# Latent tokens gather U and V of a pick as one row of 8 KB; dots, GELU, weights and V sums follow two rows at a time

## The chip, the cores and the metric

One core of a Trainium2 chip. The metric is the device time of one execution in microseconds, the median of the runs.

## What is computed

One inference step of a hybrid backbone with two layers, on 128 context tokens and 256 latent tokens of width 1024, all in float32. Each layer has token mixers (pooling, a two-way state scan, differential attention) and then PEER expert retrieval: every token picks 128 experts (8 heads of 16) of 16384 by product keys, reads for each pick a row of U and a row of V of 4 KB each, and adds a gated sum to its state.

```
act = jnp.einsum("td,thkd->thk", xb, u_tab[ib])
return jnp.einsum("thk,thkd->td", jax.nn.gelu(act) * gb, v_tab[ib])
```

The rows read for this are 3 tiles of 128 tokens x 128 picks x 2 layers x 8 KB, 805 MB in all; the weights, keys and inputs are 163 MB more.

## The kernel before

The program runs four steps k = 0 to 3: context of layer 0, latents of layer 0 (two tiles of 128 tokens), context of layer 1, latents of layer 1. Each step has a dense part (projections, mixers, attention, output projection, query projection `wq`), then the choosing of the picks (`choose` on DVE: MAX8, FIND_INDEX8, MATCH_REPLACE8, lines 1460 to 1566), which ends in the index tables `idx` and `vidx`. The gathers of a step run beside the dense part and the choosing of the next step, those of the last step alone at the end.

A **U gather** (line 695, GpSimd, called POOL here) takes column r of `idx`: 128 rows of 4 KB, partition p getting the row for pick r of token p. DVE then multiplies it with `h_kept` (the 128 hidden states of the tile, copied to PSUM at line 1866) and sums along the row (line 1871), which gives one column of `dots`. After 64 columns ACT applies GELU (line 1367) and DVE multiplies with the gates into `wv`, regrouped in 16 pieces (line 1882).

A **V gather** uses `vidx`, in which the index table is regrouped (line 1571, 16 copies of 32x32) so that the four quarters of the partitions hold four picks of the same 32 tokens. For 16 such gathers DVE spreads the weights over a 128x512 tile `vw` (line 1852); PE then multiplies each gathered tile, in two halves of 512 columns, with a 128x32 slice of `vw` (line 1077). Four gathers of a unit belong to four groups of 32 tokens, so that their outputs lie in the four lanes of 32 partitions of `acc[0]` and `acc[1]`. After all 128 picks DVE adds `acc` to x (lines 1895 to 1900), which lets the next layer begin.

A matmul in float32 appears as two MATMUL records; a 128x512 one of line 1077 as two records of 128*32, 128x512.

The order of all this is written out: a plan (`gather_plans`) gives each pause of the dense part a list of events. For the latents `events_two` interleaves "u" (4 U gathers), "v" (4 V gathers, 19 units behind) and "g", "w", "s", "x" for the GELU, the weights, the `vw` tile and the end. Every engine walks the same list between its dense pieces, and POOL issues the gathers in that order. Each gather goes to a slot of 4 KB per partition: 10 in `ring`, and others where other buffers are free, so that beside the context step of layer 1 there are 17, and at the end 34 and more. A slot is given again only after its last user: a U slot after its dot (`u_used`), a V slot after its two matmuls (`v_used`).

```
if held_before[n] is not None:
    before = stream[held_before[n]]
    pool.wait_ge(u_used if before[0] == "u" else v_used, used_after[before])
table, at = (io["peer_u"], idx) if kind == "u" else (io["peer_v"], vidx)
```

SyncE (SP) loads the weight chunks of 2 MB, 16 KB per partition, on its own queue.

## Time and profile before

| | us |
|---|---|
| median of 3 runs | 2434.72 |
| lowest and highest | 2434.61, 2435.57 |
| span of the profiled execution | 2689.8 |
| PE, DVE, POOL, ACT busy in the profile | 1510.1, 1524.4, 1466.1, 281.3 |

The profile gives the span from the first to the last instruction and no time of its own for what lies around it. The profiled execution is 255 us longer than the median. The page slices its span in 40 parts with the busy share of the engines and of the 16 DMA engines; a share of DMA somewhat above 1.00 can stand in a short window, since packets are counted with their overlap.

### The profile page before, as it was taken

The numbers are of one execution on the slowest core, as the hardware profiler recorded it, in microseconds if no ns is written. First come the engines' busy times: TensorE is split into PE (matmuls) and PEld (weight loads), VectorE is DVE, ScalarE is ACT, GpSimd is POOL, SyncE is SP. The second block draws the span as 40 slices with busy tenths as digits, with TensorE's granted clock in tenths as the row PEclk, the third lists the DMA queues.
The fourth block names the chain that finished last, engine by engine and source line by source line (L and its number), as shares of the span: only waits on it lengthen the run. The fifth ranks groups of instructions, "written<-read, shape, count | busy, mean of one in ns | idle before, by whom it ended". The sixth has DMA issues, their size and how long they took to land.

```text
span 2689.8 us, 20637 instructions
## 1 busy us (share of the span) xinstructions
PE 1510.1 (56%) x6676; PEld 682.0 (25%) x6676; DVE 1524.4 (57%) x4059; ACT 281.3 (10%) x715; POOL 1466.1 (55%) x1540
## 2 busy tenths in 40 slices
PE   6898668694244554554556866868400444442466
PEld 2464433371012110122312442354100100110012
DVE  0349974756886555455360965575776844446401
ACT  1321133010000110100000032211000000000000
POOL 0005445536665666666556635545676666667664
PEclk8889888896666665676768787878755655565568
DMA  9979998988999999999979988888899999999997
GB/s 360 411 320 379 395 388 324 365 306 318 357 397 411 412 388 379 371 410 411 389 286 374 364 341 314 324 313 296 318 399 373 343 383 375 358 374 383 378 357 271
DMA packets 238044, 969.43 MB, mean 360 GB/s; under 512 B 26314, under 2 KB 28746, under 8 KB 227954
## 3 DMA queue, kind: packets, MB, share of 16 engines
q0 software_dynamic: 221184, 805.40, 78.0%
q1 hardware_dynamic: 16754, 162.71, 14.9%
q8 instruction: 54, 0.88, 0.1%
q14 instruction: 52, 0.43, 0.0%
HBM read 964.87 MB, written 3.15 MB: 360 GB/s over the span
## 4 chain that ended last, share of the span: by engine, by line
DVE 27%; PE 24%; issue 15%; POOL 13%; another core or an unknown queue 11%; DMA 7%; ACT 2%; SPq 0%; DVEq 0%; ACTq 0%; POOLq 0%
PE acc L1077 8%; PE psum L1031 6%; DVE ring L1871 6%; POOL work L695 6%; POOL ring L695 5%; DVE work L1871 3%; PE psum L786 3%; DVE work L1463 2%; POOL wring L695 2%; DMA ring<-peer_v_in,vidx 2%; PE psum L796 2%; DVE work L1460 2%; DMA ring<-peer_u_in,idx 1%; DVE wring L1871 1%
## 5 line engine op out<-in xcount | busy, mean ns | idle before, releaser
L695 POOL DMA_INDIRECT ring<-peer_u_in,idx x415 | 396.5, 955 | 460.6 <-DVE idx L1566 208.0
L1871 DVE CUSTOM_DVE_ANT_0 ring<-ring,h_kept 128x1024 f32<-128x1024 f32 x415 | 488.9, 1218 | 126.3 <-DMA ring<-peer_u_in,idx 93.5
L695 POOL DMA_INDIRECT ring<-peer_v_in,vidx x392 | 378.5, 966 | 325.8 <-PE acc L1077 116.9
L1077 PE MATMUL acc<-ring,vw 128*32 128x512 f32 x1412 | 299.2, 778 | 276.6 <-DVE vw L1852 107.6
L1077 PE MATMUL acc<-work,vw 128*32 128x512 f32 x852 | 218.4, 794 | 325.5 <-DVE vw L1852 155.0
L1871 DVE CUSTOM_DVE_ANT_0 work<-work,h_kept 128x1024 f32<-128x1024 f32 x220 | 262.0, 1219 | 159.3 <-DMA work<-peer_u_in,idx 124.2
L695 POOL DMA_INDIRECT work<-peer_v_in,vidx x267 | 252.0, 944 | 144.8 <-issue 74.0
L695 POOL DMA_INDIRECT work<-peer_u_in,idx x220 | 207.1, 941 | 116.7 <-issue 58.9
L1031 PE MATMUL psum<-work,wring 128*128 128x256 f32 (+1 forms) x896 | 187.1, 369 | 49.5 <-issue 46.6
L786 PE MATMUL psum<-wring,work 128*128 128x512 f32 (+1 forms) x432 | 180.4, 575 | 32.4 <-issue 22.8
L1031 PEld LDWEIGHTS psum<-work,wring 128*128 128x128 f32 x896 | 160.3, 216 | 81.5 <-issue 62.0
L1077 PEld LDWEIGHTS acc<-ring,vw 128*32 128x32 f32 x1412 | 59.9, 127 | 461.5 <-issue 366.6
L1077 PEld LDWEIGHTS acc<-work,vw 128*32 128x32 f32 x852 | 45.6, 130 | 474.1 <-issue 426.1
L1119 ACT ACTIVATE work<-psum 128x512 f32<-128x512 f32 (+3 forms) x224 | 92.8, 428 | 684.3 <-remote 320.8
L786 PEld LDWEIGHTS psum<-wring,work 128*128 128x128 f32 x432 | 83.9, 211 | 130.2 <-issue 118.5
L1871 DVE CUSTOM_DVE_ANT_0 wring<-wring,h_kept 128x1024 f32<-128x1024 f32 x68 | 81.4, 1220 | 54.8 <-DMA wring<-peer_u_in,idx 25.1
L1460 DVE MAX8 work<-work 128x8 f32<-128x128 f32 (+1 forms) x288 | 52.5, 253 | 103.5 <-ACT work L1119 93.0
L1007 PE MATMUL psum<-wring,work 128*128 128x512 f32 x192 | 88.5, 622 | 3.2 <-ACT work L1294 3.2
L774 PE MATMUL psum<-const,hn 128*128 128x128 f32 x96 | 18.4, 357 | 116.8 <-DVE hn L1448 75.4
L1077 PE MATMUL acc<-ring,work 128*32 128x512 f32 x156 | 55.0, 794 | 49.0 <-issue 32.3
L695 POOL DMA_INDIRECT wring<-peer_u_in,idx x68 | 66.9, 983 | 25.7 <-issue 20.1
L796 PE MATMUL psum<-work,wring 128*128 128x256 f32 (+1 forms) x288 | 61.1, 369 | 31.5 <-issue 17.0
(244 smaller groups left out, 2028.4 us busy)
## 6 DMA issues: line engine op xcount, KB each, us to landing
wring<-w_in_in SPq DMA_DIRECT2D x17, 2048.0 KB
wring<-peer_wq_in SPq DMA_DIRECT2D x14, 2048.0 KB
wring<-mod_w_in SPq DMA_DIRECT2D x10, 2048.0 KB
ring<-mod_w_in SPq DMA_DIRECT2D x9, 2048.0 KB, 12.2
wring<-w_out_in SPq DMA_DIRECT2D x8, 2048.0 KB
work<-mod_w_in SPq DMA_DIRECT2D x5, 2048.0 KB, 14.4
ring<-peer_u_in,idx POOLq DMA_INDIRECT x415
ring<-peer_v_in,vidx POOLq DMA_INDIRECT x392
```

Source lines behind the costliest of these rows:

```text
L695: nc.gpsimd.indirect_dma_start(slots[slot_of[n]], None, table, bass.IndirectOffsetOnAxis(ap=at[:, col + r:col + r + 1], axis=0))\
L774: ins = tr(p[:, i * P:(i + 1) * P], hn[st.X + t][:, b * P:(b + 1) * P], ident)
L786: ins = mm(p[:, 0:n], st.L.hT[0][:, b, t * P:(t + 1) * P], w[:, b, slot:slot + n], start=(b == 0), stop=(b == DB - 1))
L796: ins = mm(p[:, 0:st.N], w[:, b, i * P:(i + 1) * P], st.L.hT[0][:, b, 0:st.N], start=(b == 0), stop=(b == DB - 1))
L1007: ins = mm(p[:, :], st.L.catT[:, b, t * P:(t + 1) * P], chunk("wo", k, cc)[:, b, :], start=(b == 0), stop=(b == DB - 1))
L1031: ins = mm(p[:, 0:N], chunk("wq", k, b // 4)[:, kb, (b % 4) * P:(b % 4 + 1) * P], st.L.hT[1][:, kb, 0:N], start=(kb == 0), stop=(kb == DB ...
L1077: ins = mm(acc[half][lane:lane + QUAD, :], w[:, at:at + QUAD], two[j - pair][0][:, half * CHUNK:(half + 1) * CHUNK], start=(r == 0), stop= ...
L1119: A(dst, src, ACT.Copy, scale=scale).then_inc(*take(*key))
L1460: d(V.max(top[:, b * TOPK + 8 * r:b * TOPK + 8 * r + 8], values[:, b * width:(b + 1) * width]))
L1463: d(V.max_index(index[:, b * TOPK + 8 * r:b * TOPK + 8 * r + 8], top[:, b * TOPK + 8 * r:b * TOPK + 8 * r + 8], values[:, b * width:(b + 1 ...
L1871: V.tensor_tensor_reduce(held, held, h_kept[:, :], 1.0, 0.0, ALU.mult, ALU.add, dots[:, dots_at(k, t) + r:dots_at(k, t) + r + 1]).then_inc ...
```

## The change

The tables U and V lie interleaved in HBM as `peer_uv`, and are seen as rows of 4 KB (`peer_one`) or as rows of 8 KB that hold U and V of one expert (`peer_both`). Context tokens go on as before with rows of 4 KB, with doubled indices. Latent tokens use a new kind of gather, "f": 128 rows of 8 KB, in a wide slot of two neighbouring old slots, indexed by `vidx`, in which now 32 columns in turn belong to one group of 32 tokens (`by_group`). A gather so holds four picks of each of the 32 tokens of a group. For the dots the hidden states of the group have to lie in all four quarters: PE spreads them by a matmul with a repeated unit matrix (`spread_h`, event "h", once in 32 gathers). Two gathers (DUO) are handled together: two dots, a GELU on 128x2 (event "e"), the weights and a `vw` piece of 128x64 (event "m", `weigh`), and four matmuls (event "p"), which take the two halves of each row to two lanes of `acc`. The event order for a tile is now f(2i), m(i-1), p(i-1), f(2i+1), e(i). A wide slot is given again after its matmuls.

Core of the diff (what is left out are the changes of names, of constants' layout and of the wide-slot bookkeeping):

```diff
+DUO = 2
+DUOS = PICKS // DUO
+VW_DUOS = SHARE // DUO
+BESIDE_CHOOSING, BEHIND_CONTEXT = 13, 10
...
+        wide = {n: ring[:, n * D:(n + 2) * D] for n in range(0, RING, 2)}
...
+        spare_line(region(10288, 3 * D), 3, after_step[STEPS - 3], after_step[STEPS - 2])
+        spare_line(region(10288 + 3 * D, 4 * D), 4, after_step[STEPS - 3], row_no["u", STEPS - 2, 0, 0])
+        spare_line(region(2 * D, 8 * D), 8, after_step[STEPS - 2], row_no["u", STEPS - 2, 0, 0])
+        for held in wring:
+            spare_line(held, DB * CHUNK // D, row_no["f", STEPS - 1, 0, 0], len(stream))
+        spare_line(region(0, 16 * D), 16, after_step[STEPS - 1], len(stream))
...
+                if kind == "f" and r == 0:
+                    pool.wait_ge(*after("both_indexed", k, t))
...
+                for before in (stream[m] for m in held_before[n]):
                     pool.wait_ge(u_used if before[0] == "u" else v_used, used_after[before])
-                table, at = (io["peer_u"], idx) if kind == "u" else (io["peer_v"], vidx)
+                at = idx if kind == "u" else vidx
                 nc.gpsimd.indirect_dma_start(
-                    slots[slot_of[n]], None, table,
+                    row(kind, k, t, r)[0], None, io["peer_both" if kind == "f" else "peer_one"],
...
+            def spread_h(k, t, g):
+
+                pe.wait_ge(u_used, dotted_before["f", k, t, g * QUAD])
+                if g == 0:
+                    pe.wait_ge(*after("h2", k, t))
+                group = slice(g * QUAD, (g + 1) * QUAD)
+                for half in range(2):
+                    o = slice(half * CHUNK, (half + 1) * CHUNK)
+                    ins = mm(h_kept[:, o], c("quads")[group, :],
+                             hn[steps[k].X + t][group, o], start=True, stop=True)
+                ins.then_inc(*mark("h_spread", k, t, g))
...
+                if kind == "p":
+                    if i == 0:
+
+                        pe.wait_ge(*after("acc_free", *previous_tile(steps, k, t)))
+                    pe.wait_ge(*after("vw", k, t, i))
+                    for j in range(DUO):
+                        r = i * DUO + j
+                        g, held = r // QUAD, row("f", k, t, r)[0]
+                        for half in range(2):
+                            lane = QUAD * ((g + 2 * half) % 4)
+                            ins = mm(acc[half][lane:lane + QUAD, :], vw_duo(i)[:, j * QUAD:(j + 1) * QUAD],
+                                     held[:, D + half * CHUNK:D + (half + 1) * CHUNK],
+                                     start=(r % QUAD == 0), stop=(r % QUAD == QUAD - 1))
+                        ins.then_inc(v_used, 1)
...
+                if kind == "e":
+                    at = dots_at(k, t) + i * DUO
+                    act.wait_ge(u_used, dotted_before["f", k, t, (i + 1) * DUO - 1] + 1)
+                    A(dots[:, at:at + DUO], dots[:, at:at + DUO], ACT.Gelu_apprx_tanh).then_inc(*mark("gelu", k, t, i))
...
+            def weigh(k, t, i):
+
+                at, place = dots_at(k, t) + i * DUO, slice(i * DUO, (i + 1) * DUO)
+                dve.wait_ge(*after("gelu", k, t, i))
+                d(V.tensor_tensor(wv[:, place], dots[:, at:at + DUO], gates_of(k, t)[:, place], ALU.mult))
+                settle()
+                if i >= VW_DUOS:
+                    dve.wait_ge(v_used, used_after["f", k, t, (i - VW_DUOS + 1) * DUO - 1])
+                else:
+                    dve.wait_ge(v_used, sums_of(*previous_tile(steps, k, t)) if t == 0 else
+                                used_after["f", k, t - 1, PICKS - (VW_DUOS - 1 - i) * DUO - 1])
+                spread_out = [P, DUO, QUAD]
+                V.tensor_tensor(vw_duo(i).rearrange("p (g t) -> p g t", t=QUAD), quad.unsqueeze(1).broadcast_to(spread_out),
+                                wv[:, place].unsqueeze(2).broadcast_to(spread_out), ALU.mult).then_inc(*mark("vw", k, t, i))
...
+                elif kind == "f":
+                    held, landed, count = row("f", k, t, i)
+                    dve.wait_ge(landed, count)
+                    at = dots_at(k, t) + i
+                    V.tensor_tensor_reduce(held[:, 0:D], held[:, 0:D], h_kept[:, :], 1.0, 0.0, ALU.mult, ALU.add,
+                                           dots[:, at:at + 1]).then_inc(u_used, 1)
+                elif kind == "m":
+                    weigh(k, t, i)
...
+    events = []
+    for n in range(st.T * DUOS + 1):
+        t, i = divmod(n, DUOS)
+        before = (st.k, *divmod(n - 1, DUOS))
+        if t < st.T:
+            if i * DUO % QUAD == 0:
+                events.append(("h", st.k, t, i * DUO // QUAD))
+            events.append(("f", st.k, t, i * DUO))
+        if n:
+            events += [("m", *before), ("p", *before)]
+        if n and n % DUOS == 0:
+            events.append(("x", st.k, t - 1, 0))
+        if t < st.T:
+            events += [("f", st.k, t, i * DUO + 1), ("e", st.k, t, i)]
+    return events
+
+
+EARLY = 30
...
-            dots = max(n for n, event in enumerate(left) if event[0] == "u") + 1
-            most = dots + int((len(left) - dots) * ROOM)
+            ends = [n + 1 for n, event in enumerate(left) if event[0] == "p"]
+            dots, most = ends[-1 - BESIDE_CHOOSING - BEHIND_CONTEXT], ends[-1 - BEHIND_CONTEXT]
```

### Where instructions move

POOL, gathers of the latents of layer 0 beside the dense part of the next context step. Before (`ring` and `work` are the slots):

```order
L695 DMA work<-peer_u_in,idx 128x1024 [waits u_used] x3
L695 DMA work<-peer_v_in,vidx 128x1024 [waits u_used]
L695 DMA work<-peer_v_in,vidx 128x1024 [waits v_used] x3
L695 DMA ring<-peer_u_in,idx 128x1024 [waits v_used]
L695 DMA ring<-peer_u_in,idx 128x1024 [waits u_used] x3
L695 DMA ring<-peer_v_in,vidx 128x1024 [waits u_used]
L695 DMA ring<-peer_v_in,vidx 128x1024 [waits v_used] x3
```

and now:

```order
L734 DMA ring<-peer_uv_in,vidx 128x2048 [waits v_used,both_indexed]
L734 DMA ring<-peer_uv_in,vidx 128x2048 [waits v_used] x4
L734 DMA work<-peer_uv_in,vidx 128x2048 [waits v_used] x3
L734 DMA ring<-peer_uv_in,vidx 128x2048 [waits v_used] x5
L734 DMA work<-peer_uv_in,vidx 128x2048 [waits v_used] x3
```

Rows of 128x1024 in 17 slots have become rows of 128x2048 in eight wide ones (five in `ring`, three in `work`), and each waits for `v_used`, so for matmuls, where every second run of four waited for `u_used` alone.

DVE, choosing in the context step of layer 1 (lines 1460 to 1502 before, 1531 to 1579 now, are the choosing itself). Before:

```order
L1882 TENSOR_TENSOR wv<-dots,gates 32x16 [waits v_step,gelu]
L1882 TENSOR_TENSOR wv<-dots,gates 32x16 x15
L1852 TENSOR_TENSOR vw1<-const,wv 128x512 [waits v_used,v_step]
L1460 MAX work<-work 128x8 x16
L1463 MAX_INDEX work<-work 128x8 [waits v_step]
L1463 MAX_INDEX work<-work 128x8 x15
L1495 TENSOR_TENSOR work<-work,const 128x256 [waits v_step]
L1502 TENSOR_TENSOR work<-work 128x8x16
```

and now, the same stretch:

```order
L1531 MAX work<-work 128x8 x16
L1534 MAX_INDEX work<-work 128x8 [waits v_step]
L1534 MAX_INDEX work<-work 128x8 x15
L1940 TENSOR_TENSOR wv<-dots,idx 128x2 [waits gelu,v_step]
L1948 TENSOR_TENSOR vw0<-const,wv 128x64 [waits v_used,v_step]
L1968 ISA ring,dots<-ring,h_kept 128x1024 [waits row_landed8]
L1968 ISA dots 128x1
L1968 ISA ring,dots<-ring,h_kept 128x1024 [waits row_landed0]
L1968 ISA dots 128x1
L1940 TENSOR_TENSOR wv<-dots,idx 128x2 [waits gelu]
L1948 TENSOR_TENSOR vw0<-const,wv 128x64 [waits v_used,v_step]
...
L1572 TENSOR_TENSOR work<-work,const 128x256
L1579 TENSOR_TENSOR work<-work 128x8x16
```

The choosing had only the weights of V units between its pieces; now it has dots (line 1968), weights (1940) and `vw` pieces (1948) of 13 duos.

PE, in the dense part of the same step, V sums between two projections. Before:

```order
L1077 MATMUL acc0<-work,vw0 32x512 [waits row_landed14,row_landed13]
L1077 MATMUL acc0<-work,vw0 32x512
L1077 MATMUL acc1<-work,vw0 32x512 x2
L1077 MATMUL acc0<-work,vw0 32x512 [waits row_landed16,row_landed15]
```

and now:

```order
L1122 MATMUL acc0<-work,vw0 32x512 [waits vw]
L1122 MATMUL acc1<-work,vw0 32x512
L1122 MATMUL acc0<-work,vw0 32x512
L1122 MATMUL acc1<-work,vw0 32x512
L1122 MATMUL acc0<-ring,vw0 32x512 [waits vw]
L1122 MATMUL acc1<-ring,vw0 32x512
L1122 MATMUL acc0<-ring,vw0 32x512
L1122 MATMUL acc1<-ring,vw0 32x512
```

A unit of four gathers was eight matmuls that filled four lanes in turn; a duo is four matmuls that alternate between two lanes, and it waits for `vw` each time instead of for the landing of rows.

## Rows read from the trace of the kernel before

**Rows 1.** The page's parts 1 to 3, whole span.
```profile
span 2689.8 us, 20637 instructions
...
PE 1510.1 (56%) x6676; PEld 682.0 (25%) x6676; DVE 1524.4 (57%) x4059; ACT 281.3 (10%) x715; POOL 1466.1 (55%) x1540
...
DMA  9979998988999999999979988888899999999997
...
q0 software_dynamic: 221184, 805.40, 78.0%
q1 hardware_dynamic: 16754, 162.71, 14.9%
```

**Rows 2.** Windows: stretch, its length, busy us per engine, clock, DMA share, GB/s.
```profile
core 0: us, PE busy (x) PEld busy (x) DVE busy (x) ACT busy (x) POOL busy (x), PEclk, DMA share, GB/s
70.00:100.00 30.00, 25.99 (x173) 14.14 (x171) 10.55 (x49) 12.86 (x27) 0.00 (x0) 0.94 1.01 430
690.00:1300.00 610.00, 289.61 (x1243) 119.72 (x1242) 371.53 (x743) 49.40 (x128) 391.40 (x413) 0.64 1.00 393
1334.00:1400.00 66.00, 30.17 (x182) 7.71 (x176) 51.49 (x264) 2.76 (x5) 34.34 (x35) 0.72 0.83 310
1400.00:1456.00 56.00, 43.41 (x152) 15.18 (x150) 3.36 (x11) 4.10 (x10) 37.99 (x41) 0.86 0.95 359
1480.00:1940.00 460.00, 326.14 (x1414) 180.40 (x1418) 309.41 (x950) 80.70 (x205) 231.36 (x241) 0.80 0.85 323
1985.00:2015.00 30.00, 0.00 (x0) 0.00 (x0) 18.21 (x30) 0.00 (x0) 22.69 (x25) 0.50 1.03 409
1940.00:2690.00 750.00, 284.65 (x1056) 65.42 (x1048) 371.68 (x691) 3.70 (x8) 487.37 (x513) 0.60 0.94 363
```

**Rows 3.** DMA view, 70 to 100 us: loads of 16 KB rows by SP.
```profile
DMA packets 883, 12.89 MB, mean 430 GB/s; under 512 B 96, under 2 KB 96, under 8 KB 96
```

**Rows 4.** DMA view, 1985 to 2015 us: gathers alone.
```profile
DMA packets 3372, 12.28 MB, mean 409 GB/s; under 512 B 376, under 2 KB 376, under 8 KB 3371
```

**Rows 5.** Timeline of POOL, 2232 to 2243 us: start, duration.
```profile
2234.67 0.94 POOL L695 DMA_INDIRECT work<-peer_v_in,vidx  x1 [0.30 <-issue]
2241.14 0.94 POOL L695 DMA_INDIRECT work<-peer_v_in,vidx  x1 [5.54 <-issue]
```

**Rows 6.** Waits, 2000 to 2690 us: total, times, longest.
```profile
POOL work L695 <- remote: 47.4, 17, 6.1
```

**Rows 7.** DVE groups in the choosing, 1334 to 1400 us: busy, mean ns.
```profile
L1571 DVE COPY vidx<-idx 32x32 uint32<-32x32 uint32 x16 | 3.0, 188 | 0.5
L1882 DVE TENSOR_TENSOR wv<-dots,gates 32x16 f32<-32x16 f32 x16 | 2.9, 180 | 0.6
L1852 DVE TENSOR_TENSOR vw<-const,wv 128x512 f32<-128x512 f32 x3 | 2.1, 692 | 0.1
```

**Rows 8.** Timeline of DVE: dots that follow one another.
```profile
2225.88 1.22 DVE L1871 CUSTOM_DVE_ANT_0 work<-work,h_kept 128x1024 f32<-128x1024 f32 x1
...
2227.16 1.22 DVE L1871 CUSTOM_DVE_ANT_0 wring<-wring,h_kept 128x1024 f32<-128x1024 f32 x1
```

**Rows 9.** DVE groups, whole span, nearest to a 128x64 product.
```profile
L1502 DVE TENSOR_TENSOR work<-work 128x64 f32<-128x64 f32 (+6 forms) x35 | 5.7, 228 | 0.0
```

**Rows 10.** Gathers issued from 1334 to 1456 us.
```profile
L695 POOL DMA_INDIRECT work<-peer_v_in,vidx x38: 935/941/1293, 1334.1 to 1444.9; - x38
L695 POOL DMA_INDIRECT ring<-peer_v_in,vidx x36: 937/941/2171, 1342.9 to 1454.5; - x36
```

**Rows 11.** V sums on PE, 854 to 860 us: ns min/median/max.
```profile
L1077 PE MATMUL acc<-ring,vw x20: 592/592/1062, 854.4 to 858.4; 128*32 128x512 f32 x20
```

**Rows 12.** Timeline of PE: two projections of the context step.
```profile
757.37 15.67 PE L786 MATMUL psum<-wring,work 128*128 128x512 f32 x32 [2.20 <-issue]
```

**Rows 13.** ACT: the GELU and its table loads, whole span.
```profile
L1367 ACT ACT_TABLE_LOAD x8 | 10.3, 1283 | 0.1
...
L1367 ACT ACTIVATE dots<-dots 128x64 f32<-128x64 f32 x12 | 3.1, 257 | 588.5 <-issue 445.2 <-DVEq L1876 143.3
```

More of the change, by code:

```diff
@@ L348, in dots_at, with vw_duo, gates_of @@
             return (sum(st.T for st in steps[:k]) + t) % 2 * PICKS
-        vw_places = [held[:, :] for held in vw] + [region(16384 + i * CHUNK, CHUNK) for i in range(2)]
         def vw_of(k, t, q):
-            return vw_places[q % (4 if k == STEPS - 1 else 2)]
+            return vw[q % 2]
+        def vw_duo(i):
+            at = i % VW_DUOS * DUO * QUAD
+            return vw[0][:, at:at + DUO * QUAD]
+        def gates_of(k, t):
+            at = (steps[k].X + t) * PICKS
+            return idx[:, at:at + PICKS].bitcast(F32)
         def job(pe, *key):
@@ L1354, in gather @@
             def gather(kind, k, t, i):
[L1355 removed]
+                if t == 0 and (kind, i) in (("v", (PICKS - SHARE) // UNIT), ("p", (PICKS - SHARE) // DUO)):
                     if k:
@@ L1861, in gather @@
                 col = n * PICKS
-                if kind == "u":
+                if kind == "h":
+                    if i == 0:
+                        dve.wait_ge(*after("picked", k, t))
+                        settle()
+                        by_group(lambda out, j, m: d(V.tensor_copy(out, gates[QUAD * j:QUAD * (j + 1), col + m:col + PICKS:4])),
+                                 gates_of(k, t), 0)
+                        settle()
+                    dve.wait_ge(*after("h_spread", k, t, i))
+                elif kind == "f":
[6 more added lines that the diff above has]
+                    weigh(k, t, i)
+                elif kind == "u":
                     if i == 0:
```

140 lines of the change are left out of this document (68 added, 72 removed).

## The prediction

> **What bounds the kernel now.** I read the page first: the DMA engines are at 9 tenths in nearly all 40 slices, PE, DVE and POOL at 55 to 57%, ACT at 10%, and of 969 MB the gathers (queue q0) are 805 [rows 1]. So bytes over the DMA rate is the first thing to price. The windows then say where that holds [rows 2]. Beside the dense part of the layer 1 context step (690 to 1300 us) DMA is at 1.00 and moves 393 GB/s: bound by DMA. While that step chooses its picks (1334 to 1400) it is at 0.83, and after it at 0.95. From 1480 to 1940, the dense part of the last step, it is at 0.85 with PE at 326 of 460 us: bound by the dense chain, which starts when the latents of layer 0 are summed. From 1940 on (the latents of layer 1, nothing beside them) it is at 0.94 with 363 GB/s. So time taken out of the layer 0 latents brings the last step forward, and time taken out of the last gathers brings the end forward; both are on the path.
>
> The profiled execution is 2689.8 us, the median 2434.72. At the mean rate of the runs (969 MB in 2435 us, 398 GB/s) DMA has few idle stretches left, fewer than the profile shows. I work out the change from the profile's durations and set it against both.
>
> **Packets.** SP's loads run at 430 GB/s: 883 packets, 787 of them of 8 KB or more, 12.89 MB, so 16 KB each [rows 3]. Gathers of 4 KB rows alone run at 409 GB/s [rows 4]. The ratio is 1.051. I read it as a fixed part per packet: a 16 KB packet carries a quarter of that part per byte, so three quarters of it are 5.1% and all of it is 6.8% of the time of 4 KB; 8 KB takes away half, 3.4%. The latents' rows are 4 tiles x 128 gathers x 128 rows x 8 KB = 537 MB, 1313 us at 409 GB/s. **-45 us**, between 0 (if a row goes as two packets) and -64 (if 8 KB moves like 16 KB). A wide gather then takes 1.049 MB / 423 GB/s = 2.48 us, two old ones 2.56.
>
> What the page on DMA of the Trainium skill (DMA: Bandwidth & Descriptors, SWDGE vs HWDGE vs iDMA) says speaks against this term: a packet is preferably at most 4096 B. By that rule the term would be 0. The 16 KB packets [rows 3] don't keep to it on SP's queue; for POOL's queue no row shows it, and I keep it as a rival.
>
> **POOL.** It issues a gather every 1.24 us (0.94 and 0.30 between) and DMA moves 4 KB rows in 1.28, so it never gets far ahead, and after a pause such as the one of 5.54 us [rows 5] nothing is queued. Pauses of this kind fall on 17 waits, 47.4 us, in the last 690 us [rows 6]. Half as many issues let POOL run ahead to the limit of the slots. The median has no room for many such pauses, so I credit **0** here, with -40 as the far end.
>
> **Choosing in the layer 1 context step.** The order puts 13 duos of dots and weights between its pieces on DVE; before it had 16 weight products and 3 `vw` tiles, 2.9 + 2.1 = 5.0 us [rows 7]. A duo is two dots at 1.28 (2225.88 to 2227.16) [rows 8], a weight product of 0.18 as in [rows 7], a 128x64 `vw` piece of 0.23 by the nearest form [rows 9], and some 0.3 for the two waits between them: 3.3 us. So the 66 us become 66 + 43 - 5 = 104, in which only 26 wide gathers, 64 us, come free. Behind it stand 20 more, 8 of them prefetched; 12 x 2.48 = 30 us. 134 us from the start of the choosing to the first gather of the next step. Before, 38 + 36 gathers were issued from 1334.1 to 1454.5, and the next step's first at 1456: 122 us [rows 10]. **+12 us**, between 0 (if the 14 us in which DVE was idle there [rows 2] take up the dots) and +38 (all that DVE gains in work).
>
> **Slots.** Beside the dense part there were 17 slots, a turn of 17 x 1.28 = 21.8 us. A unit of four V gathers holds its first slot for 3 x 1.28 us and a PE unit (16 records of 592 ns in four lanes, 2.4 us [rows 11]): some 6 us. A U slot is held for one dot. Now 8 wide slots give a turn of 19.8 us, and the first gather of a duo waits for its partner (2.5), for the first gather of the next duo (2.5), a dot (1.3), GELU and weights (1.0) and PE: eight records of 592 ns in two lanes are 2.4 us, at the lower clock (records of 1062 ns, [rows 11]) 4.2. That is 10 to 11 us. What DVE or PE may be away without a gap in DMA falls from some 14 to some 8 us (a POOL issue taken off both). A projection is 7.8 us (two in 15.67, [rows 12]), just inside; at the lower clock, or with a wait for ACT before it, it is not. I take one gap of 1 us at some 10 of the 20 pauses: **+10 us**; the ends are 0 and 20 x 2.3 = +45.
>
> **Small terms.** The first gather of a latent tile now waits for `vidx`, 3.0 us of copies [rows 7]; twice, and at the 0.85 of the last step's windows about half of it shows: +3 (0 to +6). At the end the last gather is followed by dot, GELU, weights and a PE duo (1.3 + 0.4 + 0.7 + 2.4) where one PE unit of 2.4 stood: +3. The 16 spreads of h are four records of some 0.6 us each on PE; DVE waits for them about 3 us once in 32 gathers, while it works 3.3 us of each 4.96: 0. GELU goes from 12 calls of 64 columns to 256 of 2 and 4 of 64, at 0.26 us or less, and the order has ten more table loads of 1.28 us [rows 13]: 13 us on an engine that is 10% busy, 0, at most +5. PE needs 2.4 to 4.2 us for a duo of 4.96, so it hides; without any sharing of lanes at the lower clock a duo would be 8 x 1.06 = 8.5 us, but where PE was busy 26 of 30 us the granted clock was 0.94, and 0.50 where it did nothing (70 and 1985 us in [rows 2]); at the upper one that duo is 4.7.
>
> **Sum:** -45 + 0 + 12 + 10 + 3 + 3 = -17 us. On the median 2435 - 17 = **2418 us**; the profiled span would be near 2673.
>
> **The rivals.**
> *A, the forecast*, 2400 to 2429 us: 0.42.
> *B, the gain is larger*: POOL's headroom brings back idle DMA time beside the packet gain. For it: 6% of 750 us are idle in the last stretch [rows 2], 45 us, with 34 slots to run ahead in. Against it: the runs are 255 us shorter than the profile, so most of that idle belongs to the profiled execution. With 35 us of it: 2383 us. 0.17.
> *C, slower, slots turn too slowly*: place, the dense part of the layer 1 context step and its choosing. Each of some 20 pauses of PE or DVE costs 2.3 us (+45 in place of +10), and the dots in the choosing cost 25 in place of 12: -45 + 45 + 25 + 6 = +31, 2466 us. It decides from the point where a wide slot is held for more than about 12 us and DMA falls below 0.93 in that stretch. For it: every wide slot waits for PE, where half the old ones waited for a dot. Against it: DMA at 1.00 there with PE at 290 and DVE at 372 of 610 us. 0.23.
> *D, it does not do what it says*: POOL cuts the 8 KB rows in packets of 4 KB. The waits stay and the packet gain is gone: +28, 2463 us. For it only the page's rule above. 0.05.
> *E, gain and waits cancel* within 5 us: 2435 us. 0.13.
>
> A measurement of this kernel can tell about 0.2%, 5 us, from no change. Faster by more: A and B, **0.59**; within it: E, **0.13**; slower: C and D, **0.28**. The likeliest is A, so **2418 us**. Its own range is 2400 to 2429; for 8 in 10 the range goes down to B's value and up to most of C's, 2380 to 2460.
>
> **What would show it.** In the profile after: POOL near 1024 indirect DMAs, 512 of them of 8 KB packets, and a packet count of q0 lower by 65,536 and the small ones of 512 gathers; if it isn't, D. In a stretch of wide gathers alone DMA should move 420 to 425 GB/s. DVE waiting for `h_spread` should stay under 50 us in all. The choosing of the layer 1 context step should last about 104 us in place of 66, with DMA near 0.65 there: if it is still 0.83, the term of +12 is wrong. Beside that step's dense part DMA at 0.97 or more is A; 0.93 or less with POOL waiting for `acc` is C. If the last 240 wide gathers come at 2.5 us each and the profiled span falls by more than 60 us, B's idle time came back in the profile, and the median tells whether it was real outside it.

## The result, and the profile after

| | us |
|---|---|
| before, median of 4 runs in this comparison | 2434.66 (2432.07 to 2435.57) |
| after, median of 4 runs | 2463.91 (2462.55 to 2470.68) |
| ratio, 95% interval | 1.0128 (1.0114 to 1.0143) |
| span of the profiled execution of after | 2463.4 |

The change makes the kernel 29 us slower where the forecast was 17 us faster; the value lies outside the range of 2380 to 2460.

The kernel before takes 2431 to 2435 us in some series of runs and 2691 to 2692 in others (one chip gave 2432 in one series and 2691 in a later one), and the profile that the prediction read [rows 1 to 13] is of the second kind, while the runs it was to forecast are of the first. A profile of the same kernel before, taken again in a series of the first kind, is the one to compare with. The profile page, parts 1 to 3, of before (that second profile):

```profile
span 2432.2 us, 20637 instructions
...
PE 1423.7 (59%) x6676; PEld 614.0 (25%) x6676; DVE 1525.2 (63%) x4059; ACT 282.1 (12%) x715; POOL 1463.7 (60%) x1540
...
DMA  9988999999999999999999999998999999999997
GB/s 367 405 342 342 409 419 409 411 414 383 405 413 412 412 409 410 409 411 412 412 411 365 410 413 386 409 416 338 406 410 409 409 409 409 409 409 410 409 409 286
```

and of after:

```profile
span 2463.4 us, 20933 instructions
...
PE 1674.9 (68%) x6740; PEld 667.5 (27%) x6740; DVE 1570.1 (64%) x4471; ACT 344.0 (14%) x973; POOL 977.2 (40%) x1028
...
DMA  8989999999999899899997999999999999999996
GB/s 358 400 341 352 410 418 409 413 411 386 414 416 423 324 409 413 361 421 391 404 366 270 392 413 389 391 412 362 384 419 422 422 421 421 422 421 422 422 421 273
...
q0 software_dynamic: 147456, 805.37, 80.5%
```

POOL has 1028 instructions for 1540 and q0 147,456 packets for 221,184 [rows 1] with the same bytes, so the rows do go as packets of 8 KB. The slices from the 31st on, but for the last, show the gain, a steady 421 to 422 GB/s for 409. Slices 14 to 23 show the loss: 324, 361, 366 and 270 among them, where before has 409 to 412 but for one slice of 365. That is the layer 0 latents beside the context step of layer 1.

Windows by stage, before (second profile): from the first layer 0 latent gather to the first MAX8 of the choosing, from there to the sum x_new, from there to the first layer 1 latent gather, and to the end. Columns as in [rows 2]. (A DMA share of 1.02 or 1.03 is what full looks like in these windows, long ones too.)

```profile
626.20:1237.20 611.00, 290.40 (x1330) 121.29 (x1330) 373.10 (x744) 52.68 (x136) 411.62 (x437) 0.64 1.02 411
1237.20:1359.60 122.40, 82.39 (x400) 17.63 (x400) 56.09 (x276) 6.46 (x14) 82.88 (x83) 0.74 0.98 386
1359.60:1748.70 389.10, 310.61 (x1412) 170.94 (x1412) 319.93 (x971) 82.12 (x207) 241.35 (x249) 0.85 1.00 396
1748.70:2432.00 683.30, 239.54 (x1056) 30.63 (x1052) 362.78 (x676) 3.59 (x8) 480.98 (x512) 0.57 1.00 399
```

The same stages of after:

```profile
626.70:1260.70 634.00, 416.14 (x1536) 141.26 (x1538) 341.98 (x841) 82.02 (x245) 204.35 (x218) 0.79 0.97 399
1260.70:1405.40 144.70, 79.44 (x228) 19.31 (x226) 106.04 (x386) 12.48 (x37) 48.96 (x51) 0.79 0.82 321
1405.40:1795.20 389.80, 308.51 (x1412) 172.10 (x1412) 320.14 (x971) 83.53 (x208) 237.10 (x245) 0.86 0.99 393
1795.20:2463.00 667.80, 377.63 (x1087) 68.43 (x1084) 388.46 (x882) 28.82 (x132) 239.59 (x256) 0.75 0.98 408
```

+23.0, +22.3, +0.7 and -15.5 us, with +0.5 ahead of them: 31 us, the difference of the spans. The third stage is the same in both, so what the layer 0 latents lose moves the end one for one.

How much of that is idle DMA? I compare each stage with the time its bytes need at the rates of undisturbed stretches, an estimate: rows of 4 KB at 409 GB/s, rows of 8 KB at 422, the rest at the 430 of [rows 3]. The DMA view of 1900 to 2000 us in before and in after gives those rates for gathers alone:

```profile
DMA packets 11239, 40.95 MB, mean 409 GB/s; under 512 B 1248, under 2 KB 1248, under 8 KB 11236
```

```profile
DMA packets 5789, 42.17 MB, mean 422 GB/s; under 512 B 643, under 2 KB 643, under 8 KB 643
```

And the two queues' bytes in the dense stage, in before (627 to 1237 us) and in after (627 to 1260 us):

```profile
q0 software_dynamic: 61952, 225.59, 92.6%
q1 hardware_dynamic: 2738, 24.71, 9.7%
```

```profile
q0 software_dynamic: 31364, 227.42, 87.3%
q1 hardware_dynamic: 2736, 24.68, 9.5%
```

Before: 225.59 MB at 409 are 552 us, 25.0 MB of weights and small ones at 430 are 58, together 610 of 610 us: nothing lost. After: 227.42 MB at 422 are 539 us, and 58, together 597 of 633: 36 us lost. The same sum for both layer 0 stages (worked out from the packets of each size in the stretch) is what the experiments below are judged by:

| lost DMA time, us | dense stage | choosing up to x_new |
|---|---|---|
| before | 0.3 | 6.8 |
| after | 35.9 | 34.3 |

What after waits for in its dense stage (waits, 627 to 1260 us: total, times, longest):

```profile
POOL ring L734 <- PE acc L1122: 290.8, 89, 17.2
PE acc L1122 <- DVE vw L1948: 200.9, 72, 12.8
POOL work L734 <- PE acc L1122: 105.3, 49, 9.0
DVE wv L1940 <- ACT dots L1433: 36.3, 9, 10.4
DVE ring L1968 <- PE h_kept L1101: 18.8, 4, 6.3
```

POOL waits for slots, whose release waits for PE, which waits for the weights from DVE. In before PE's longest waits in that stage (627 to 1237 us) are for DMA, for rows of V:

```profile
PE acc L1077 <- DMA work<-peer_v_in,vidx: 131.9, 29, 38.3
PE acc L1077 <- DMA ring<-peer_v_in,vidx: 126.5, 38, 14.4
```

One of the gaps, in the timeline of after at 803 to 849 us, shows the links of the chain one by one:

```profile
817.01 6.76 DVE L1769 SCALAR_TENSOR_TENSOR work<-work,par 128x128 f32<-128x128 f32 x24
823.69 1.21 DVE L1968 CUSTOM_DVE_ANT_0 work<-work,h_kept 128x1024 f32<-128x1024 f32 x1
...
826.44 1.92 PE L1122 MATMUL acc<-ring,vw 128*32 128x512 f32 x4 [12.75 <-DVE vw L1948]
...
828.65 0.94 POOL L734 DMA_INDIRECT ring<-peer_uv_in,vidx  x1 [13.35 <-PE acc L1122]
...
830.00 3.78 PE L1101 MATMUL h_kept<-hn,const 32*128 32x512 f32 x4
...
833.82 1.22 DVE L1968 CUSTOM_DVE_ANT_0 ring<-ring,h_kept 128x1024 f32<-128x1024 f32 x1 [6.29 <-PE h_kept L1101]
...
838.99 8.30 PE L825 MATMUL psum<-wring,work 128*128 128x512 f32 x16
...
847.33 0.60 ACT L1186 ACTIVATE work<-psum 128x512 f32<-128x512 f32 x1 [19.56 <-PE psum L825]
847.82 0.20 ACT L1433 ACTIVATE dots<-dots 128x2 f32<-128x2 f32 x1
848.04 0.16 DVE L1940 TENSOR_TENSOR wv<-dots,idx 128x2 f32<-128x2 f32 x1 [10.39 <-ACT dots L1433]
```

DVE does 12 us of its dense piece without a dot (its previous work for a gather ended at 811.7), so PE has no weights and POOL no slot for 13 us; then DVE waits for the spread of h, and then a GELU stands in ACT's order behind the copy of a projection, which waits for PE: 10.4 us more for DVE. The row whose dot starts at 833.82 here had landed at 820.1 and its last matmul ended at 849.6 (the landings, dots and matmuls of the trace, counted in order), so it held its slot for 29.5 us after landing.

### The profile page after: what moved, and what is told of

It reads as the page before. It is cut to its first block, busy times and chain, and to the rows that moved or that the text cites. A ratio compares the mean times of both kernels' runs of the same rounds, so it can differ in the third digit from the quotient of the medians.

```text
span 2463.4 us, 20933 instructions
## 1 busy us (share of the span) xinstructions
PE 1674.9 (68%) x6740; PEld 667.5 (27%) x6740; DVE 1570.1 (64%) x4471; ACT 344.0 (14%) x973; POOL 977.2 (40%) x1028
## 3 DMA queue, kind: packets, MB, share of 16 engines
q0 software_dynamic: 147456, 805.37, 80.5%
## 4 chain that ended last, share of the span: by engine, by line
DMA 41%; DVE 25%; PE 24%; issue 5%; ACT 3%; POOL 1%; SPq 0%; DVEq 0%; POOLq 0%; ACTq 0%
DMA ring<-peer_uv_in,vidx 18%; DMA work<-peer_uv_in,vidx 12%; PE acc L1122 6%; DMA wring<-peer_uv_in,vidx 6%; PE psum L825 5%; DVE ring L1981 4%; PE psum L835 2%; DVE work L1534 2%; PE psum L1070 2%; DVE work L1531 2%; DMA ring<-peer_uv_in,idx 2%; PE psum L1046 1%; DVE work L1539 1%; PE acc L1144 1%; PE acc L751 1%
## 5 line engine op out<-in xcount | busy, mean ns | idle before, releaser
L734 POOL DMA_INDIRECT ring<-peer_uv_in,vidx x401 | 382.7, 954 | 605.7 <-PE acc L1122 469.4
L1122 PE MATMUL acc<-ring,vw 128*32 128x512 f32 x924 | 309.4, 803 | 278.5 <-DVE vw L1948 278.5
L1122 PE MATMUL acc<-work,vw 128*32 128x512 f32 x876 | 295.4, 797 | 190.5 <-DVE vw L1948 190.5
L734 POOL DMA_INDIRECT work<-peer_uv_in,vidx x256 | 245.5, 959 | 311.6 <-PE acc L1122 257.6
L734 POOL DMA_INDIRECT ring<-peer_uv_in,idx x193 | 183.3, 950 | 341.1 <-DVE idx L1644 208.3
L1433 ACT ACTIVATE dots<-dots 128x2 f32<-128x2 f32 x256 | 52.0, 203 | 1120.3 <-DVE dots L1968 1120.2
L1070 PE MATMUL psum<-work,wring 128*128 128x256 f32 (+1 forms) x896 | 164.9, 347 | 3.0 <-ACT work L1186 3.0
L1144 PE MATMUL acc<-ring,vw 128*32 128x512 f32 x680 | 115.6, 725 | 52.6 <-DMA ring<-peer_uv_in,vidx 34.6
L1122 PE MATMUL acc<-wring,vw 128*32 128x512 f32 x248 | 91.1, 858 | 69.5 <-DVE vw L1948 69.5
L734 POOL DMA_INDIRECT wring<-peer_uv_in,vidx x62 | 58.1, 937 | 94.8 <-PE acc L1122 89.6
L1940 DVE TENSOR_TENSOR wv<-dots,idx 128x2 f32<-128x2 f32 x256 | 40.2, 157 | 58.4 <-ACT dots L1433 58.3
## 6 DMA issues: line engine op xcount, KB each, us to landing
wring<-w_in_in SPq DMA_DIRECT2D x17, 2048.0 KB, 10.8
wring<-peer_wq_in SPq DMA_DIRECT2D x14, 2048.0 KB, 10.4
wring<-mod_w_in SPq DMA_DIRECT2D x10, 2048.0 KB, 13.3
```

Source lines behind the costliest of these rows:

```text
L734: nc.gpsimd.indirect_dma_start(row(kind, k, t, r)[0], None, io["peer_both" if kind == "f" else "peer_one"], bass.IndirectOffsetOnAxis(ap=a ...
L1070: ins = mm(p[:, 0:N], chunk("wq", k, b // 4)[:, kb, (b % 4) * P:(b % 4 + 1) * P], st.L.hT[1][:, kb, 0:N], start=(kb == 0), stop=(kb == DB ...
L1122: ins = mm(acc[half][lane:lane + QUAD, :], vw_duo(i)[:, j * QUAD:(j + 1) * QUAD], held[:, D + half * CHUNK:D + (half + 1) * CHUNK], start= ...
L1144: ins = mm(acc[half][lane:lane + QUAD, :], w[:, at:at + QUAD], two[j - pair][0][:, half * CHUNK:(half + 1) * CHUNK], start=(r == 0), stop= ...
L1433: A(dots[:, at:at + DUO], dots[:, at:at + DUO], ACT.Gelu_apprx_tanh).then_inc(*mark("gelu", k, t, i))
```

## Experiments

The runs stand in four series of four kernels, each on one chip with the kernel before among them; ratios are to that kernel in the same series. Series 1 and 4 are of the kind of the result (before 2431.6 and 2431.1 us); in series 2 and 3 before takes 2691.8 and 2691.4. Theory S says that the wide slots of the layer 0 latents turn too slowly, theory C that the choosing starves DMA because every row now needs DVE.

### The kernel before, profiled again (series 1)

No edit.

> The kernel before, unchanged, once more. The first profile of it was 255 us longer than its runs, with PE records 1.4 us apart and POOL pauses of 5.5 us, while the profile of the changed kernel (2463.4 us) agrees with its own runs. All theories: an undisturbed profile has a span near 2433 us. Theory S (the wide slots of the layer 0 latents turn too slowly) and theory C (choosing starves DMA, because every row now needs DVE): beside the dense part of the layer 1 context step DMA stands at 0.99 or more, and while that step chooses at 0.9 or more, where the changed kernel has 0.96 and 0.70; together it has some 10 to 15 us of idle DMA time from the first layer 0 latent gather to the first gather of the next step, the changed kernel 52 us. Rival P (the gain by 8 KB rows is not there): the old gathers alone move 420 GB/s or more.

Measured: one run, 2434.05 us, span 2432.2. DMA is at 1.02 in the dense stage and 1.02 while it chooses:

```profile
1237.20:1290.90 53.70, 30.14 (x152) 4.11 (x152) 50.96 (x262) 2.14 (x3) 36.59 (x35) 0.70 1.02 408
```

Lost DMA time is 7 us against 70 in the changed kernel, and the old gathers alone move 409 GB/s, so rival P falls. There is no POOL pause: in the waits from 2000 to 2350 us the largest of POOL with nothing to wait for is 0.3 us in this profile (first row) and 5.5 in the one I predicted from (second row):

```profile
POOL work L695 <- issue: 36.3, 119, 0.3
```

```profile
POOL work L695 <- issue: 34.0, 86, 5.5
```

### Wide rows only for the latents of layer 1 (series 1)

```diff
-                each = 1 if st.lat else 2
+                each = 1 if k == STEPS - 1 else 2
...
-            left = events_two(steps[k])
-            plan["exp", 1] = plan["exp", 1] + left[:EARLY]
-            left = left[EARLY:]
+            left = events_two(steps[k]) if k == STEPS - 1 else events_apart(steps[k])
+            early = EARLY if k == STEPS - 1 else 8
+            plan["exp", 1] = plan["exp", 1] + left[:early]
+            left = left[early:]
...
-            ends = [n + 1 for n, event in enumerate(left) if event[0] == "p"]
-            dots, most = ends[-1 - BESIDE_CHOOSING - BEHIND_CONTEXT], ends[-1 - BEHIND_CONTEXT]
+            dots = max(n for n, event in enumerate(left) if event[0] == "u") + 1
+            most = dots + int((len(left) - dots) * ROOM)
```

`events_apart` is the old `events_two`.

> Only the latents of layer 1 use rows of 8 KB, those of layer 0 are gathered as before (U rows and V rows of 4 KB, 19 units apart, 17 slots). Theories S and C: all of the loss sits in the layer 0 latents, and the packet gain of the last 256 wide gathers (0.08 us each, 20 us) stays: 2435 - 20 = 2415 us, between 2408 and 2422, faster than both kernels. Rival T (the loss is in the last step or in something common, as GELU by twos, the spreads of h, coarser waits of the vw tiles): 2440 to 2460 us. Rival P (no packet gain): 2435.

Measured: 2420.5 us, ratio 0.9957 (0.9945 to 0.9969): faster than both kernels, by 11 and 43 us. The layer 0 stages are those of before again, 613.1 and 119.2 us, and the last one is 670.2:

```profile
625.90:1239.00 613.10, 293.47 (x1338) 123.17 (x1338) 373.14 (x744) 52.71 (x136) 411.72 (x437) 0.63 1.03 411
1239.00:1358.20 119.20, 79.69 (x400) 17.33 (x392) 55.99 (x277) 6.48 (x14) 81.64 (x83) 0.76 0.99 388
...
1747.80:2418.00 670.20, 387.50 (x1084) 70.37 (x1084) 388.62 (x882) 28.70 (x132) 239.43 (x256) 0.73 0.98 407
```

So the packet gain is real, and all of the loss belongs to the layer 0 latents. Rivals T and P fall.

### GELU of the layer 0 latents left out (series 1)

```diff
-                if kind == "e":
+                if kind == "e" and k != 1:
...
-                dve.wait_ge(*after("gelu", k, t, i))
+                if k == 1:
+                    dve.wait_ge(u_used, dotted_before["f", k, t, (i + 1) * DUO - 1] + 1)
+                else:
+                    dve.wait_ge(*after("gelu", k, t, i))
```

> The GELU of the layer 0 latents is left out; the weights then wait only for the dots, not for ACT. Under theory S in the form that I read in the profile of after (ACT walks its list in order, so a GELU stands behind the copy of a projection, which waits for PE, and DVE waited 10.4 us for it at 848 us): half of the 25 us of idle DMA time in the dense part goes, 2450 us (2445 to 2455). If PE's projection alone holds the slots, GELU or not: 2460 to 2464. Theory C alone: 2462.

Measured: 2454.96 us, ratio 1.0099 (1.0085 to 1.0114), at the edge of what I expected, and the mechanism is not borne out at its size: the dense stage is 630.2 us with 32.6 lost (from 35.9), a tenth of its loss where I had said half, and the choosing up to x_new 141.1 (29.7, from 34.3). GELU behind ACT's copies is a real part, 7 us by the ratios and 9 by the medians, and a small one.

### Slots given again after the dot (series 1)

```diff
-                    pool.wait_ge(u_used if before[0] == "u" else v_used, used_after[before])
+                    if before[0] == "f" and before[1] == 1:
+                        pool.wait_ge(u_used, dotted_before[before] + 1)
+                    else:
+                        pool.wait_ge(u_used if before[0] == "u" else v_used, used_after[before])
...
+                        if k == 1:
+                            held = None
+                            other = hn[steps[k].X + t]
...
+                                     other[:, half * CHUNK:(half + 1) * CHUNK] if k == 1 else
                                      held[:, D + half * CHUNK:D + (half + 1) * CHUNK],
```

> In the layer 0 latents the V sums read the hidden states in place of the gathered V half, and a wide slot is given again after its dot (so V sums of these tokens are left out in effect; all instructions are still issued). Theory S: the 25 us of idle DMA beside the dense part mostly go, since a slot no longer waits for GELU, weights and PE: 2440 to 2446 us. Theory C: DVE is what starves DMA, in the dense part too, and dots are still in DVE's order: 2458 to 2463 us.

Measured: 2437.8 us, ratio 1.0023 (1.0014 to 1.0032). The dense stage is 610.0 us with 10.8 lost (from 35.9), the choosing up to x_new 142.1 with 32.6 lost (from 34.3). The two losses are different things: holding the slot through GELU, weights and PE makes 25 of the 36 us in the dense stage and hardly any of the second. PE's work is not the limit by itself: it is busy 406 us of the stage here and 416 in the changed kernel (290 before), and the 25 us come back all the same. Of the 11 us that are left the waits say that POOL waits for dots (238 and 150 us in all); that DVE being away in its dense pieces makes them is the reading, not tested by itself.

### Six wide slots in place of eight (series 2 and 4)

```diff
-                slot = min((i for i in free if i in wide), key=lambda i: max(last_held(i), last_held(i + 1)))
+                slot = min((i for i in free if i in wide and not (stream[n][1] == 1 and i in (13, 15))), key=lambda i: max(last_held(i), last_held(i + 1)))
```

> The layer 0 latents get six wide slots in place of eight (two of the three in the work buffer are left unused). Theory S (in the dense part a wide slot is held while DVE or PE do their dense pieces): a pause that now costs nothing up to about two slots more begins to cost, up to 5 us at each of some 20 pauses: 2464 + 50 = 2514 us (2490 to 2560). Theory C alone (only DVE's work while choosing counts): 2464 to 2470, since DVE is the limit there, not the slots.

Measured in series 2, where before takes 2692 us: 2703.87 us, ratio 1.0048 (1.0024 to 1.0071), against 0.9702 of the changed kernel in series 3. And in series 4, where before takes 2431:

> Six wide slots for the layer 0 latents in place of eight. It cost 91 us where before takes 2692 us (2704 against 2613). Where before takes 2432 us: theory S 2464 + 50 to 80, some 2530 us, ratio 1.04, nearly all of it before the choosing starts. Rival (it is slots times slow issues that cost there): under 2490, ratio under 1.024.

Measured: 2563.14 us, ratio 1.0539 (1.0523 to 1.0556): 99 us over the changed kernel, more than expected. The lost time is 124.1 us in the dense stage and 51.1 in the second. So two slots of 2.48 us each cost 88 us over the dense stage's 20 and more pauses, 44 us a slot. From six to eight slots the curve is steep, and at eight 36 us are still lost. Whether a ninth or tenth slot would bring them back was not run.

### More and fewer duos beside the choosing (series 2 and 4)

```diff
-BESIDE_CHOOSING, BEHIND_CONTEXT = 13, 10
+BESIDE_CHOOSING, BEHIND_CONTEXT = 20, 10
```

and with 26, 4 and 0, 10.

> No duo beside the choosing: its 13 go to the dense part, 10 stay behind. Theory C: 13 x 1.66 = 22 us more, 2486 us; the choosing lasts about 65 us, with DMA idle for some 45 of them. Rival (the dots in the choosing are what the change costs there, without them it is as before): 2450 us or less.

> 20 duos beside the choosing of the layer 1 context step in place of 13, 10 behind as before, so 7 fewer in the dense part. Theory C with a price (a duo costs the dense part 4.96 us of DMA, and DVE in the choosing 3.3): 7 x 1.66 = 12 us less, 2452 us. Rival (the 26 rows that the choosing has already come too late for their slots, more only lengthens it): 2464 or more.

> 26 duos beside the choosing and 4 behind it, so 7 fewer in the dense part and 6 fewer behind. Theory C: 13 x 1.66 = 22 us less, 2442 us; the choosing would last about 150 us and DMA stand near 0.9 in it. Rival as for 20 and 10: 2464 or more.

Measured, all in series 2, where before takes 2692 us: 2641.17 (0.9808, 0.9776 to 0.9841), 2599.56 (0.9656, 0.9628 to 0.9684), 2588.39 us (0.9609, 0.9578 to 0.9640). The forecasts in us were for the other kind of series and can't be set against these; the steps between them can: from 0 to 20 duos 41.6 us, 2.1 per duo for the 1.66 expected. Again in series 4:

> 26 duos beside the choosing and 4 behind it, for the chip on which before takes 2432 us. There the changed kernel loses 28 us more than before in the choosing and behind it. Theory C: 13 duos x 1.66 us = 22 less than the changed kernel, 2442 us, ratio 1.004. Rival (it was a gain only where issues are slow, 25 us there): 2460 or more, ratio 1.012. Where before takes 2692 us: 2589 again.

Measured: 2439.85 us, ratio 1.0029 (1.0017 to 1.0041), 24 us under the changed kernel. The two layer 0 stages are 594.5 and 165.0 us, with 28.2 and 22.1 lost. The windows of the choosing alone, from the first MAX8 to the gates, in the changed kernel and in this one:

```profile
1260.70:1344.10 83.40, 37.48 (x100) 6.79 (x98) 76.11 (x314) 4.88 (x15) 18.92 (x19) 0.71 0.74 281
```

```profile
1218.30:1345.20 126.90, 63.30 (x196) 12.63 (x194) 107.35 (x384) 8.23 (x28) 43.46 (x44) 0.77 0.97 391
```

With 13 duos DVE is busy 76 of 83 us and DMA at 0.74: too few gathers stand beside DVE's work. With 26, DMA is at 0.97. A duo adds 2.4 us of DVE work there ((107.35 - 76.11) / 13) and 4.96 of DMA, so more duos cover the choosing's own work, where 13 leave DMA idle. By bytes over rate 28.0 us are lost between the first MAX8 and the gates with 13 duos, 9.5 with 26, and 0.3 in before.

### The dots beside the choosing left out (series 4)

```diff
+                    if (k, t) == (1, 1) and 83 <= i < 109:
+                        dve.sem_inc(u_used, 1)
+                        return
```

> The 26 dots (line 1968) of the rows beside the choosing are left out; their gathers, weights and V sums stay. Theory C in the form that DVE's work is the limit in the choosing: 26 x 1.22 = 32 us of DVE work go, and the 26 rows then need 64 us of DMA in a choosing of about 75: 2464 - 27 = 2437 us, ratio 1.002 (where before takes 2692: 2613 - 27 = 2586). Rival: not the work of DVE, but the slots that wait for GELU, weights and PE between pieces of the choosing: 2455 or more, ratio 1.0095 or more.

Measured: 2443.06 us, ratio 1.0060 (1.0037 to 1.0082), 17 us under the changed kernel by the ratios and 21 by the medians; between the two forecasts and nearer to theory C; the choosing to the gates falls from 83.4 to 67.7 us, the whole second stage from 144.7 to 127.7, its loss from 34.3 to 18.1:

```profile
1254.10:1321.80 67.70, 35.80 (x100) 7.30 (x98) 49.17 (x266) 5.07 (x16) 17.89 (x19) 0.73 0.87 340
```

DVE's dots are half of that loss, not all of it. A part of the other half stands in POOL's waits. The first gather behind those that stand beside the choosing goes to a slot in `work` and waits for the gates, the last piece of the choosing. That wait, in after (1261 to 1405 us):

```profile
POOL work L734 <- DVE gates L1667: 15.2, 1, 15.2
```

In before it is 2.0 us. In after POOL stands from 1329.2 to 1344.4 us, and DMA moves nothing in the last 8 us before the gates. The same wait is 9.9 us with the dots left out and 7.3 with 26 duos. No run takes this wait away by itself, so its price is not shown.

### Both costs taken down (series 3 and 4)

The edits of the slots given after the dot and of 26, 4 together.

> Both suspected costs taken down at once: the V sums of the layer 0 latents read the hidden states, so that a slot is given again after its dot (their V sums are left out in effect), and 26 duos beside the choosing, 4 behind. Theories S and C as two separate terms: 2438 - 22 = 2416 us where before takes 2432, below the kernel before. Rival (one cause with two names, DVE's order): no more than 5 us under the better of the two alone, 2433 us or more.

In series 3, where before takes 2691 us: 2560.05 us, ratio 0.9514 (0.9491 to 0.9538), 53 us under the changed kernel there. In series 4:

> Slots given again after the dot (V sums of the layer 0 latents left out in effect), with 26 and 4 duos. Where before takes 2432 us: two separate terms, 2438 - 22 = 2416, ratio 0.994. Rival, one cause with two names: 2433 or more, ratio 1.0005 or more. Where before takes 2692 us: 2560 again (there 2613 fell by 24 with 26 and 4 duos, and by 29 more with the slots).

Measured: 2416.52 us, ratio 0.9943 (0.9930 to 0.9957). Against the 1.0128 of the change, the slots alone take 1.05%, the 26 and 4 duos 0.99%, both 1.85%: nearly additive (2.04% for the sum), two terms. The losses are 2.4 and 13.3 us. POOL's waits in its dense stage now end with DVE's dots:

```profile
POOL ring L737 <- DVE dots L1975: 237.3, 115, 13.4
```

### The changed kernel where before takes 2692 us (series 3)

No edit for the first; the other two are the kernels of above.

> The changed kernel itself, to have it on the same chip as the three runs beside it. The first four kernels ran where the kernel before takes 2432 us, the second four where it takes 2692 us (and its profile, as the one I predicted from, shows PE records 1.4 us apart and POOL pauses of 5.5 us with nothing to wait for). Where before takes 2432: 2464 us, ratio 1.013. Where before takes 2692: choosing with 0, 20 and 26 duos gave 2641, 2600 and 2588 there, so 13 duos give about 2614, ratio 0.971: the change would be faster there, because POOL's pauses between issues cost half as much with half the issues (rival B of the prediction). If instead the ratio is 1.013 there too, the pauses have nothing to do with the change.

> Wide rows only for the latents of layer 1. Where before takes 2432: 2420 as measured, 43 us less than the changed kernel. Where before takes 2692: the last 673 us are 749 there in the kernel before, and 668 in the wide ones, so 2692 - 78 = 2614 us, near the changed kernel; the layer 0 part would then be even between the two schemes there (771 us from the first latent gather to the next step before, 755 with 20 duos, some 770 with 13).

> 26 duos beside the choosing and 4 behind it. Theory C (a duo costs the dense part 4.96 us of DMA and the choosing 3.3 us of DVE): 22 us less than the changed kernel on the same chip, 2442 where before takes 2432, and some 25 less where it takes 2692. Rival (the slow issue alone made it a gain): no less than the changed kernel where before takes 2432.

Measured: 2613.26 us, ratio 0.9702 (0.9677 to 0.9727); 2615.34 (0.9713, 0.9682 to 0.9744); 2588.73 (0.9613, 0.9586 to 0.9640). The sign of the change turns. By the windows of that series' profile of after, against the profile of before that stood in the prediction, cut at the same events (both below, before first):

```profile
685.80:1334.40 648.60, 313.91 (x1384) 133.69 (x1380) 382.28 (x766) 52.52 (x136) 415.87 (x439) 0.65 1.00 393
1334.40:1476.30 141.90, 83.11 (x378) 25.71 (x370) 56.12 (x277) 6.48 (x14) 86.01 (x89) 0.79 0.90 334
...
1941.00:2690.00 749.00, 283.65 (x1046) 65.25 (x1044) 370.78 (x688) 3.70 (x8) 486.68 (x512) 0.60 0.94 363
```

```profile
686.80:1327.30 640.50, 416.07 (x1560) 141.84 (x1554) 352.12 (x861) 82.62 (x246) 206.66 (x218) 0.80 0.96 395
1327.30:1473.20 145.90, 81.79 (x228) 19.79 (x226) 106.01 (x386) 12.48 (x37) 48.95 (x51) 0.75 0.82 321
...
1941.40:2614.00 672.60, 372.15 (x1080) 67.94 (x1076) 396.08 (x893) 28.82 (x132) 241.89 (x256) 0.76 0.97 404
```

In the last stage before needs 749 us where it needs 683 in the other kind of series, while after needs 673 and 668. In the two layer 0 stages before has already lost 54 us there (28.4 and 26.0), after 77 (42.7 and 34.5). The third stage takes 465 and 468 us in place of 389 and 390, so that both kernels pay 76 to 78 us there.

## Why the prediction was wrong

**Packets, -45: right in kind, -35 in size.** The rate of a stretch of wide gathers is 422 GB/s, inside the 420 to 425 forecast; on the 1313 us of the prediction that would be -40 (1313 x (1 - 409/422)). The prediction's own sum took 5.1% of the shorter time for a share of the longer, which is 4.9%; rightly worked out it gives -43. The two layer 0 stages need 18 us less at full rate (726 to 708) and the rows of the last one land in 653 us for 670, 17 less. Rival D is false by the packet count. The Trainium skill (DMA: Bandwidth & Descriptors, SWDGE vs HWDGE vs iDMA) prefers packets of at most 4096 B. The runs here went the other way: rows of 8 KB, one packet each as this profile counts them, moved at 422 GB/s on POOL's queue and rows of 4 KB at 409, 3% less.

**Slots, +10: this is the step that failed.** It measured +36, inside the ends of 0 and +45 that I gave it, but 26 us over the value in the sum, the largest of its errors. The argument was that a wide slot is held for 10 to 11 us, that a turn of eight slots then leaves 8 us of slack, that a projection of 7.8 us is "just inside", and that 10 of 20 pauses would cost 1 us. The usual hold was right: where the trace shows the landing of the first row of a duo in the dense stage (55 of them), the median from there to its last matmul is 11.0 us. What failed is the step from the usual hold to the pauses: in 21 of the 55 it is over 12 us, up to 29.5. The pauses were not looked up one by one. DVE's dense piece at 811.6 to 823.7 us is 12 us long, a spread of h adds 6.3 and a GELU behind a copy 10.4, and since each duo passes DVE, ACT, DVE and PE in program order, they add up on the same slots. The slots given after the dot (-25 us in this stage) show that it is the holding, and six slots (+88) that there was no slack to give.

**Choosing, +12: the second step that failed.** Lost time went from 6.8 to 34.3 us, +27. The measure I named, from the start of the choosing to the first gather of the next step, went from 112.9 to 123.8 us, +10.9, near the forecast, but by luck, since it ends at an issue. The next step's dense part starts at x_new, and that is 9.5 us behind the first gather in before and 20.9 in after: the last V gather of before is issued at 1348.6 us and lands 7.4 us later, the last wide one at 1383.0 and lands 16.9 later. The lost time itself lies in the choosing: 28.0 us up to the gates for 0.3 in before, and 6.5 behind them for 6.6. The term set the idle time there against a profile in which before, too, lost 16 us up to the gates. The choosing took 83 us (104 forecast, from the 66 of a profile in which it took longer than the 54 of the runs, and from 3.3 us of DVE a duo for the 2.4 measured), with DMA at 0.74 (0.65 forecast). Nor did the term have the 15.2 us in which POOL waits for the gates.

**The base was the wrong kind of execution.** I saw that the profile was 255 us longer than the runs, and used this against rival B alone, while I took the stage's durations and the idle DMA in it for the runs. In that kind of execution the two terms are +22.8 us together (54.4 to 77.2 lost; 14.3 and 8.5, where I had 10 and 12), and I had said 22. In the runs before loses 7 us, so nearly the whole 70 us of after is new. A term "the slack falls from 14 to 8 us" depends on how much is lost already; I should have worked out the price once with the 26 us of idle DMA in the choosing and once with none.

**POOL, 0, with -40 as the far end: right for the runs, wrong for the profile.** Where before takes 2692 us the last stage falls by 76 us, of which some 17 are packets: rival B, larger than its 35. That POOL's headroom is the reason was argued and not tested: PE, too, has 172 us of waits for nothing visible in that stage of before and 15 in after's. Where before takes 2432 us it is 0, as its last stage moves 409 GB/s without a gap. I also wrote that the profiled span would be near 2673; in a series of that kind it is 2614.

**Small terms.** The `vidx` copies and the rest of the third stage cost 1.2 us (+3 forecast), the end 1.9 (+3): from the last landing to the end 13.3 us before and 15.2 after. DVE waited 42.8 us for `h_spread` in all, under the 50 I gave; 23.2 of it in five waits of up to 6.3 us beside the layer 1 context step, and with eight slots that need not be nothing.

**Rival C** came nearest: 2466 us, for 0.23. Its place was right; that its sum is so near is partly luck, as it had the packets at -45 for -35 and the slots at +45 for +36. Its point, DMA below 0.93 in the dense stage, was set too low: the mean is 0.97, and 36 us are lost all the same, as a share of 1.02 is the full one there. My test for A, DMA at 0.97 or more, would have called this run a success. A share is a poor test where 36 of 634 us decide; bytes over rate is a better one.

The sum in the end: -18 (packets, layer 0) + 36 + 27 + 1 - 17 (packets, layer 1) + 2 = +31, the difference of the two spans.

## What to carry to other kernels

Merging two transfers into one merges their release as well: a row that was free after one dot is then held through the whole chain to the last engine, and a long piece of work on any engine in that chain holds up its slots. Count the longest pieces against slots times transfer time before crediting the bandwidth; here the merge, with eight slots, paid where no dense part runs beside it, and using it there alone gave 2420 us. Work that needs hardly any DVE (the old V gathers) was also what filled DMA while DVE was choosing, and that is lost silently. And before taking slack from a profile, see that its span is that of the runs.

## What the runs showed of the hardware

The same program takes 2432 or 2692 us by series, on one chip in both ways, and stayed so through a series (2427.9 to 2436.0 and 2684.0 to 2708.0 over 17 runs each); the first profile, of 2689.8 us, is the one that stands beside runs of 2435. Where before takes 2692 us the wide gathers alone keep their 421 to 422 GB/s, while in before POOL pauses 5.5 us with nothing to wait for and the chain that ended last is 15% "issue" for 5%. The cause of this was not tried and stays open. What it does to the two kernels is shown: the one of few, large transfers loses less by it (673 for 668 us in the last stage) than the one that issues a gather every 1.24 us beside a DMA time of 1.28 (749 for 683), so the ratio of the same two kernels is 1.013 in one kind and 0.970 in the other. That it is the room to run ahead that spares the first was not tested. Wide rows for the last latents alone is the one version with all of its work that was faster than before in both, 0.996 and 0.971.
